# Input products of block 1 and output product of block 2 moved to 512-column matmuls, their halves added at read-out

## What is computed

```
h = rms_norm(x, pre_mix_g);  z = h @ w_in                            # block 1, input product
x_new = x + m_lat[2] * ((sig(g_a)*(o_a@w_br_a) + sig(g_b)*(o_b@w_br_b)) @ w_out)   # block 2, output product
```

## Time and profile before

| what | value |
|---|---|
| median of three runs | 3025.4 us (3024.79 to 3029.65) |
| profiled execution: device time, span | 3029.62 us, 3027.8 us |
| PE busy, matmuls | 2876.0 us (95%), 19290 |
| DVE, ACT, POOL busy | 1922.9 us (64%), 1563.5 us (52%), 797.0 us (26%) |
| DMA | 610.63 MB, mean 202 GB/s |
| `w_in` product | about 12 to 217 us of the span |
| `w_out_2` product | about 2153 to 2252 us of the span |

### The profile page before, as it was taken

The page is one execution under the profiler, slowest core; times in us unless marked ns, Lnnn a source line. Parts: engine busy times, 40 slices in busy tenths (PEclk is TensorE's granted clock), DMA queues, the critical chain, the costliest instruction groups (busy, mean ns, idle before and its releaser), DMA issues.

```text
span 3027.8 us, 54772 instructions
## 1 busy us (share of the span) xinstructions
PE 2876.0 (95%) x19290; PEld 2625.7 (87%) x19290; DVE 1922.9 (64%) x2344; ACT 1563.5 (52%) x2279; POOL 797.0 (26%) x644
## 2 busy tenths in 40 slices
PE   7998799999999999899999999989989999999999
PEld 7998789998899988788888888789978888888888
DVE  5666778666678877533355666757786665555554
ACT  5555455445577653323344666665546654344443
POOL 3455433003344422112103422234434520000000
PEclk9999899999999999999999999999999999999999
DMA  7873756667777775344556654577767876666665
GB/s 261 270 255 123 238 174 215 187 182 232 242 247 244 246 235 184 98 145 145 157 159 186 199 165 153 179 230 238 238 216 239 267 236 184 191 187 186 183 188 166
DMA packets 175403, 610.63 MB, mean 202 GB/s; under 512 B 19200, under 2 KB 28800, under 8 KB 174912
## 3 DMA queue, kind: packets, MB, share of 16 engines
q1 hardware_dynamic: 161856, 589.37, 62.1%
q10 hardware_dynamic: 12656, 16.97, 1.8%
q0 software_dynamic: 784, 2.88, 0.3%
HBM read 598.66 MB, written 5.77 MB: 200 GB/s over the span
## 4 chain that ended last, share of the span: by engine, by line
PE 71%; DVE 11%; ACT 7%; DMA 6%; issue 5%; DVEq 0%; ACTq 0%; SPq 0%; POOL 0%; POOLq 0%
PE acc L1579 20%; PE acc L1583 20%; PE acc L1581 10%; PE acc L1582 9%; DVE wlo L1021 4%; ACT whi L603 3%; DMA raw<-w_ada 2%; ACT cond_products L599 2%; PE acc L1567 1%; PE acc L1570 1%; PE acc L1569 1%; PE sums L1797 1%; PE acc L1577 1%; DVE conv_out L1116 1%; DMA raw<-w_fg 1%
## 5 line engine op out<-in xcount | busy, mean ns | idle before, releaser
L1021 DVE TENSOR_TENSOR wlo<-raw,whi 128x1024 fp32r<-128x1024 f32 x864 | 1141.1, 1331 | 884.1 <-ACT whi L603 881.9
L1583 PE MATMUL acc<-operand,wlo 128*128 128x256 f32 (+1 forms) x4848 | 1415.3, 292 | 0.0
L603 ACT ACTIVATE whi<-raw 128x1024 fp32r<-128x1024 f32 x864 | 908.8, 1057 | 978.0 <-PE acc L1583 578.0
L1581 PE MATMUL acc<-operand,whi 128*128 128x256 f32 (+1 forms) x3168 | 953.0, 301 | 79.3 <-DVE wlo L1021 46.3
L1583 PEld LDWEIGHTS acc<-operand,wlo 128*128 128x128 f32 x4848 | 934.8, 193 | 15.6
L1582 PE MATMUL acc<-operand,whi 128*128 128x256 f32 (+1 forms) x3168 | 942.7, 298 | 0.0
L1581 PEld LDWEIGHTS acc<-operand,whi 128*128 128x128 f32 x3168 | 615.3, 194 | 104.0 <-issue 47.0
L1582 PEld LDWEIGHTS acc<-operand,whi 128*128 128x128 f32 x3168 | 615.8, 194 | 13.6
L1579 PE MATMUL acc<-operand,whi 128*128 128x512 f32 x1680 | 602.1, 401 | 14.0 <-DVE operand L1354 7.7
L457 POOL TENSOR_TENSOR cond_products<-cond_products 128x512 f32<-128x512 f32 x192 | 254.3, 1325 | 1257.0 <-ACT cond_products L599 1255.6
L1579 PE MATMUL acc<-ffn_act,whi 128*128 128x512 f32 x1344 | 473.4, 396 | 4.2 <-DVE wlo L1021 4.1
(11 more groups left out here) (212 smaller groups left out, 2420.0 us busy)
## 6 DMA issues: line engine op xcount, KB each, us to landing
raw<-w_ada SPq DMA_DIRECT2D x256, 512.0 KB, 4.4
raw<-w_in SPq DMA_DIRECT2D x224, 512.0 KB, 4.1
raw<-w_up SPq DMA_DIRECT2D x176, 512.0 KB, 4.3
raw<-w_down SPq DMA_DIRECT2D x88, 512.0 KB, 4.4
raw<-w_fg SPq DMA_DIRECT2D x88, 512.0 KB, 4.2
raw<-w_fu SPq DMA_DIRECT2D x88, 512.0 KB, 4.0
raw<-w_fd SPq DMA_DIRECT2D x88, 512.0 KB, 3.6
raw<-w_o SPq DMA_DIRECT2D x32, 512.0 KB, 4.5
```

Source lines behind the costliest of these rows:

```text
L603: act.activation(whi[j % RING][:], raw[j % RING][:], ACT.Copy).then_inc(hi_done, 2 if st.entries[j % st.upb - 1] == (None, ADA_VEC) else 1)
L1021: dve.tensor_tensor(wlo[j % RING][:], raw[j % RING][:], whi[j % RING][:].bitcast(F32), ALU.subtract).then_inc(lo_done, 2 if prev[0] is Non ...
L1581: pe.matmul(out_, h[:, x, f], mov[:, 0], start=first, stop=False)
L1583: ins = pe.matmul(out_, l[:, x, f], mov[:, 0], start=False, stop=last)
```

## The change

"scale" and "out" join `WIDE`. For "scale" it adds the ACT copy of the low columns and replaces the one DVE instruction with two: add, then multiply by `RS` in place, with a wait between; since it joins `LOW_FIRST`, `lo` goes ahead of the read-out on DVE. For "out" the read-out takes two more DVE instructions (x += gate·low) ahead of `finish`. The copy of "scale" lands in the output tile itself, not in one that is `Yt` further on.

```diff
-V_STEPS = {"scale": 0, ..., "out": 4, ...}
-A_STEPS = {"conv": (2, 1), "glu": (2, 1), "down1": 1, "q": 1}
-WIDE = ("glu", "down_x", "down1", "down2", "q")
-LOW_FIRST = ("down1", "q")
+V_STEPS = {"scale": 1, ..., "out": 6, ...}
+A_STEPS = {"scale": 1, "conv": (2, 1), "glu": (2, 1), "down1": 1, "q": 1}
+WIDE = ("scale", "out", "glu", "down_x", "down1", "down2", "q")
+LOW_FIRST = ("down1", "q", "scale")
...
-                    tile = b * (2 * st.GB) + (st.tile0 + 2 * gb + Yt)
+                    tile = b * (2 * st.GB) + (st.tile0 + 2 * gb + (Yt if st.kind == "down1" else 0))
...
                     if k == "scale":
-                        dve.tensor_tensor(R[:, ds(tile, 2), :], sums, rep(RS[:], 2), ALU.mult).then_inc(evac_done, 1)
+                        y = R[:, ds(tile, 2), :]
+                        dve.wait_ge(astep, ast(st, b, gb, 0))
+                        did(dve.tensor_tensor(y, sums, y, ALU.add))
+                        settled()
+                        dve.tensor_tensor(y, y, rep(RS[:], 2), ALU.mult).then_inc(evac_done, 1)
...
-                        for part in (sums, low) if k == "down_x" else (sums,):
+                        for part in (sums, low):
...
-                                if m == 1 and part is low:
+                                if k == "down_x" and m == 1 and part is low:
                                     ins.then_inc(evac_done, 1)
...
-                    did, settled = steps_from(st, b, gb, 1 if k == "mix_out" else 2)
+                    did, settled = steps_from(st, b, gb, {"mix_out": 1, "down2": 2, "out": 4}[k])
```

More of the change, by code:

```diff
@@ L94, in __init__ @@
         assert groups % per_body == 0 and self.upb % RING == 0
-V_STEPS = {"scale": 0, "mix_out": 3, "conv": (4, 7), "down1": 0, "down2": 4, "kv": 0, "q": 0, "gate": 0,
-           "branch_a": 0, "branch_b": 1, "out": 4, "glu": (0, 3), "down_x": 3}
-A_STEPS = {"conv": (2, 1), "glu": (2, 1), "down1": 1, "q": 1}
-WIDE = ("glu", "down_x", "down1", "down2", "q")
-LOW_FIRST = ("down1", "q")
+V_STEPS = {"scale": 1, "mix_out": 3, "conv": (4, 7), "down1": 0, "down2": 4, "kv": 0, "q": 0, "gate": 0,
+           "branch_a": 0, "branch_b": 1, "out": 6, "glu": (0, 3), "down_x": 3}
+A_STEPS = {"scale": 1, "conv": (2, 1), "glu": (2, 1), "down1": 1, "q": 1}
+WIDE = ("scale", "out", "glu", "down_x", "down1", "down2", "q")
+LOW_FIRST = ("down1", "q", "scale")
 def steps(table, kind, gb):
```

## The result

The changed kernel takes 3037.5 us (median of 13 runs, 3031.5 to 3042.0); the kernel before, timed beside it, 3026.1 us (13 runs). Ratio 1.0037, 95% interval 1.0028 to 1.0045: slower by 11 us. The forecast was 3033.4, +8.0; 3037.5 lies in its range of 3028.0 to 3040.0. The profiled execution has a span of 3038.1 us, against 3027.8.

The account below looks back on a forecast made before the run. PE bounds w_in with 0.29 us to spare once per body; DVE already bounds w_out_2 at entry 10. Terms -3.2 +0.7 +1.4 +3.0 +1.0 -0.65 +4.8 +0.9 = +7.95 on 3025.4 give 3033.4 us, range 3028.0 to 3040.0.

Parts of the forecast that it names:

- Matmuls in `w_in`: In w_in, one instruction saved per product gains 0.054 us a unit over 59 units: -3.2 us.
- Start: At the first matmul of st_in, the longer group 0 read-out of st_inh is no longer hidden: +0.7 us (0.3 to 1.0).
- Bodies of `w_in`: In seven w_in bodies, POOL holds the new multiply, delaying entry 10's lo: 0.2 us each, +1.4 (bounds none to 4.9).
- Rival C: Every w_in body loses the multiply's hold, 0.7 us in place of 0.2: +3.5, 3036.9 us; chance 0.12.
- End of `w_in`: At the end of w_in, the last read-out stands behind hi and lo, delaying the attention: +3.0 us (1.3 to 4.0).
- clock, +1.0: After w_in, PE's new idle stretch brings a short lower clock in the attention's first steps: +1.0 us (0 to 9).
- `w_out_2`, −0.65 and +4.8: In w_out_2, faster matmuls gain 0.65 us; two more DVE instructions lengthen entry 10's wait 1.2 a body, +4.8 in four.
- End of `w_out_2`: At the end of w_out_2, longer read-out before the sum for the norm, with semaphores: +0.9 us.
- Rival A: In w_out_2, DVE's additions are absorbed and stalls don't grow: -2.0 us, 3023.4 us; chance 0.10.
- rival B: After w_in, the clock stays low through the attention: +9 in place of +1, 3041.4 us; chance 0.08.

Follow-up runs that it names:

- e3: Against the kernel before: both products wide, but read out as before, the high-times-low columns left out of the result; 3025.6 us, ratio 0.9997.
- e1: Against the change: only the input product (scale) wide, the output product as before; 3030.4 us, ratio 1.0017 to the kernel before.
- e4: Against the change: narrow matmuls in both products with the change's read-outs, which take the same sums a second time; 3039.5 us, ratio 1.0044 to before.
- e5: Against e1: the DVE addition writes its sum back to PSUM, so the multiply reads one operand there; 3027.7 us, ratio 1.0003 to before.
- e8: Against the change: group 0's read-outs behind entry 10's lo, input sum in PSUM, input's last group read out before the next hi and lo; 3029.3 us.
- e10: Against e8: the output product's read-out back in its place, only its group 0 finish moved late as in e9; 3024.4 us, ratio 0.9996 to before.
- e11: Against e10: output product narrow with its read-out as before, its finish still late, input product wide; 3023.6 us, ratio 0.9992 to before.
- e2: Against the change: only the output product (out) wide, the input product as before; 3031.5 us, ratio 1.0019 to the kernel before.
- e9: Against the kernel before: in w_out_2 only group 0's finish (square, two additions) moved behind the next two entries' low halves; 3022.8 us, ratio 0.9991.

## Why the prediction came out as it did

The sign and the place of every loss were right, and the total of +8.0 was low against +11.4. Two terms were mis-sized, both too small; that they came out 2.8 and 1.8 us short and the rest close is what kept the time in the range.

- **Matmuls in `w_in`, −3.2.** e3 shows −3.9 over 54 units: 0.073 us a unit, 9 ns a saved matmul, where I took 7 from the earlier trace rows. Where no wait came before, a unit takes 2.77 for 2.88, 0.347 a product and not 0.353: 0.11 saved, which over 54 units would be 5.9. In its last three bodies e3 has short waits and units of 2.83 behind them. By the 2.5 ns that the Trainium skill ("TensorE: Matmul & The Clock Gate", section "Back-to-back issue gap") gives for an isolated matmul it would be 1.1. The trace shows more, and the section itself says that this formula leaves out the weight load, of which the page counts one for each matmul here (PEld, 18522).
- **Start, +0.7.** Measured +0.7 by landmark, where the five kernels with the old code lie between −1.4 and +0.3. The trace of after shows the wait itself, on PE at the first matmul of `st_in`, which before came at 52.69 without a wait:

```profile
53.49 0.49 PE L1583 MATMUL acc<-operand,whi 128*128 128x512 f32 x1 [0.82 <-DVE tiles L1070]
```

  The four kernels with the change's read-out there (the change, e1, e4, e5) idle 0.76 to 0.83 at this place, none of the others does. So this term held, size and cause.
- **Bodies of `w_in`, +1.4: this step failed.** Measured 4.2, near my upper bound of 4.9. My own numbers didn't give the 0.2 a body that I took: a `lo` 0.3 late against a margin of 0.29 less 0.11 leaves 0.12. In the body shown, counted from the first matmul of entry 6, that `lo` ends 0.71 later than before (6.17 for 5.46), and PE reaches entry 10 0.22 sooner (two units of 2.77 for 2.88), so it waits 0.71 + 0.22 − 0.29 = 0.64. Of the 0.71, 0.55 is the length of `lo`. I had the multiply 0.2 us ahead of L463 and took that for the cheap side. It did come ahead of it, at 0.16 us, and it cost: L463 was held, then `lo`, 0.4 us each time (e5). The rest I had not in the sum: the condition entry follows a transfer that doesn't get faster with PE (0.72 behind the start of entry 6 in the mean, where it was 0.42), and PE itself comes sooner. How the rest divides between these two no run isolates. That both hang on the faster PE fits e4, which has the same read-outs and the same hold and loses 1.2. Rival C had the size, 0.7, but for the other order of the two instructions. The 4.2 and e3's −3.9 make +0.3 for a stage that measured +0.9; the 0.6 stays open.
- **End of `w_in`, +3.0, and clock, +1.0.** 66–67 is +3.8. I had add and multiply end at 221.3; they end at 222.85 in a trace that is 1.58 late at landmark 66, so at 221.3. The first exp follows at 228.70, 5.74 later than before. A stretch of clock 0.51 stands at 222 us, 6.8 us long. What it costs can't be read apart, but it is little: with the same order e1 has 10.2 us of low clock in 66–67 and e4 3.4, and they lose 3.9 and 3.7. The other order (e8, e10, e11) takes 1.4 to 3.1 of the 3.8 away.
- **`w_out_2`, −0.65 and +4.8: mis-sized.** The waits ahead of entry 10 grew by 1.3 a body, 5.2, for my 1.2. Missing were one more wait of 0.84 and a unit stretched by 1.36 at the lower clock; the units without a wait give about 1.5 back. In all +5.9 for my +4.15. The matmuls' −0.65 is −0.3 by e3.
- **End of `w_out_2`, +0.9.** Measured +0.7.

Sum of the trace: 0.7 + 0.9 + 3.8 + 5.9 + 0.7 = 12.0 for the changed stages; 0.3 between 67 and 571 and −2.0 behind 603, where the code is the same, bring it to 10.3, the difference of the two spans. Rival A (the additions absorbed) falls with e2; rival B with 66–67: the clock didn't stay low through the attention, it was back at 1.00 from 229 us on.

## What to carry to other kernels

A saved matmul is worth something only in the units in which PE doesn't wait: where another engine already ends the wait, a faster PE just waits longer (e3 in `w_out_2`), so look there first, and for an order that removes the wait before a cheaper product (e9 gained 2.8 us in its stage by moving three instructions). An operation added ahead of the conversion that PE waits for cost its whole length where PE waited already (e4 in `w_out_2`: 0.9 us a body for 0.8 us of new work), and little where PE had slack (e4 in `w_in`: 1.2 us in seven bodies). A faster PE used that slack up: price the cheaper product and its read-out together. The place in the order was worth more than the length of the work (e8, e9). When a VectorE operation with both inputs in SBUF lands next to GpSimd work, count the hold on GpSimd too, and what GpSimd then holds.

## What the runs showed of the hardware

- A multiply on DVE that never took longer than 0.69 us made GpSimd's next instruction 0.39 us longer (0.75 to 1.14) and DVE's own next one 0.4 us longer; reading one input from PSUM instead took both away.
- Wide products come at two paces in one trace at clock 1.00. In `w_out_2` twelve of them start 2180.20 to 2184.36, 0.347 us each, ten from 2186.21 to 2189.74, 0.353 each:

```profile
2180.20 0.40 PE L1583 MATMUL acc<-operand,whi 128*128 128x512 f32 x1
...
2184.36 0.40 PE L1583 MATMUL acc<-operand,whi 128*128 128x512 f32 x1
...
2186.21 0.40 PE L1583 MATMUL acc<-operand,whi 128*128 128x512 f32 x1
...
2189.74 0.40 PE L1583 MATMUL acc<-operand,whi 128*128 128x512 f32 x1
```

  What sets the pace stays open.
- After the third of four similar PE waits in `w_out_2` (2.41 us) the granted clock was 0.51 for 3.4 us; after the first two (1.75 and 2.25) it stayed up, and in the units behind the fourth (1.79) too. e2 has two such stretches in that stage (2195 and 2222 us), e9, without a wait there, none between 2153 and 2247 us. So a wait of this size can be followed by a further loss of 1.4 us. What decides it is open: in e2 the longest wait of the stage (2.20 us) was not followed by one.
